# A two-layer attention trunk on one core: mask matmuls folded into the operands, scores in equal halves, and transposes and their evacuations moved ahead of the next tile's scores

## The reference

```python
# layer 0, group A (latent heads, width 64 + 32): query chunk must not be before key chunk
mask = key_chunk[None, :] <= q_chunk[:, None]            # chunks of 64
s = jnp.where(mask[None, None], s, NEG_INF)
# layer 0, group B (chunk heads, width 64): own chunk and the 8 before it
s = jnp.where(valid[None, None, :, None, :], s + bias[None, :, None], NEG_INF)
# layer 1 (fox heads, width 64): causal by token, with a decay
s = jnp.where(mask[None, None], s + cq[..., :, None] - cum[..., None, :], NEG_INF)
# all of them
pr = jax.nn.softmax(s, axis=-1)
o = pr @ v                                               # then a SiLU gate, one output projection
```

## Time and profile before

| | us |
|---|---|
| median of 3 runs | 1913.37 (1913.27 to 1915.61) |
| the profiled execution, its time | 1913.73 |
| its span, first to last instruction | 1911.9 |
| TensorE matmul busy | 1768.6 (93%) |
| VectorE busy | 952.7 (50%) |
| ScalarE busy | 835.6 (44%) |
| GpSimd busy | 105.6 (6%) |
| DMA, share of 16 engines | 39.6% in the main queue |

### The profile page before, as it was taken

How to read it: one execution, slowest core, us unless ns; L and a number is a source line. 1 busy time by engine, 2 the same in 40 slices (tenths; PEclk the granted TensorE clock), 3 DMA queues, 4 the chain that set the end, 5 groups by cost and what they waited for, 6 DMA issues and landing times. The chain is left out here.

```text
span 1911.9 us, 31893 instructions
## 1 busy us (share of the span) xinstructions
PE 1768.6 (93%) x12720; PEld 1628.7 (85%) x12720; DVE 952.7 (50%) x1812; ACT 835.6 (44%) x1708; POOL 105.6 (6%) x58
## 2 busy tenths in 40 slices
PE   5999788899999998999979999999989999889998
PEld 5999787787887777989979999998867777789898
DVE  5454465304777774253354444421067777832521
ACT  4433233315777773142252333312168888811410
POOL 0000000000121120000000000000002121100000
PEclk9999999999999999999989999999989999999999
DMA  6045457525445555101133344453265555251211
GB/s 187 23 161 162 121 153 211 156 73 168 133 122 148 142 131 177 51 28 56 45 111 110 122 133 123 122 148 99 83 161 137 140 134 144 79 181 35 70 64 39
DMA packets 178275, 223.94 MB, mean 117 GB/s; under 512 B 12760, under 2 KB 148200, under 8 KB 178128
## 3 DMA queue, kind: packets, MB, share of 16 engines
q1 hardware_dynamic: 177056, 218.43, 39.6%
q0 software_dynamic: 640, 2.62, 0.5%
q10 hardware_dynamic: 432, 0.85, 0.1%
HBM read 150.34 MB, written 77.29 MB: 119 GB/s over the span
## 5 line engine op out<-in xcount | busy, mean ns | idle before, releaser
L1617 PE MATMUL m_acc<-g_area,g_a_hi 128*128 128x256 f32 (+1 forms) x2560 | 479.8, 288 | 10.1 <-DVE g_area L202 5.6
L1617 PEld LDWEIGHTS m_acc<-g_area,g_a_hi 128*128 128x128 f32 x2560 | 404.6, 193 | 10.4 <-DVE g_area L202 5.7
L1617 PE MATMUL m_acc<-g_area,g_a_lo 128*128 128x256 f32 (+1 forms) x1280 | 366.4, 286 | 0.0
L1617 PEld LDWEIGHTS m_acc<-g_area,g_a_lo 128*128 128x128 f32 x1280 | 245.8, 192 | 0.0
L640 PE MATMUL pa_acc<-g_area,g_a_hi 128*128 128x256 f32 (+2 forms) x1024 | 208.2, 301 | 15.9 <-DVE g_area L202 15.9
L1617 PE MATMUL t_acc<-g_area,g_a_hi 128*128 128x256 f32 x1024 | 190.1, 286 | 5.1 <-DVE g_area L202 5.1
L640 PEld LDWEIGHTS pa_acc<-g_area,g_a_hi 128*128 128x128 f32 x1024 | 167.2, 195 | 16.4 <-issue 16.4
L202 DVE TENSOR_TENSOR g_area<-g_w_raw,g_area 128x2048 fp32r<-128x2048 f32 (+5 forms) x55 | 112.0, 2050 | 123.2 <-ACT g_area L196 123.2
L1617 PEld LDWEIGHTS t_acc<-g_area,g_a_hi 128*128 128x128 f32 x1024 | 160.7, 192 | 5.3 <-DVE g_area L202 5.3
L640 PE MATMUL pa_acc<-g_area,g_a_lo 128*128 128x256 f32 (+2 forms) x512 | 151.8, 297 | 0.0
L1042 PE MATMUL ab_scores<-g_area 96*128 96x512 f32 (+5 forms) x480 | 143.6, 380 | 3.8 <-PEq L102 3.8
(11 more groups left out here) (236 smaller groups left out, 3322.1 us busy)
## 6 DMA issues: line engine op xcount, KB each, us to landing
g_w_raw<-in_fox_w_in SPq DMA_DIRECT2D x16, 1024.0 KB, 6.0
g_area<-f_q SPq DMA_DIRECT2D x48, 256.0 KB
g_area<-f_k SPq DMA_DIRECT2D x48, 256.0 KB
g_w_raw<-in_ab_w_in SPq DMA_DIRECT2D x10, 1024.0 KB, 5.6
ab_v<-s_v SPq DMA_DIRECT2D x16, 512.0 KB, 3.5
g_w_raw<-in_pe_gate_w SPq DMA_DIRECT2D x8, 1024.0 KB, 5.3
f_v<-m_pr SPq DMA_DIRECT2D x32, 256.0 KB, 2.8
fox_v<-f_v SPq DMA_DIRECT2D x16, 512.0 KB, 3.5
```

Source lines behind the costliest of these rows:

```text
L1617: last = nc.tensor.matmul(dst, a[:, k, t * P:(t + 1) * P], w[:, k0 + k, 0:n], start=(k == 0 and a is m_hi and w is w_hi), stop=(k == kt - ...
```

## The change

Five things are changed.

1. *Latent masks.* Eight rows are added to the contraction (`MROWS` = 96 + 8): a row per block of 128 tokens, in q a 1 where the query is in the first half of its block, in k a -1e30 where the key is in the second half of the same block. They come from a DRAM tensor `m_chunk`, which `stage_ab` writes: VectorE makes the rows in the tile `y`, POOL stores them with four DMAs, and VectorE waits for those stores before its first evacuation overwrites `y`. `load_qk` issues 7 loads for a latent head instead of 4.
2. *Chunk masks.* They are written into the bias: two POOL DMAs put -1e30 from `far_off` over the corners of `s_bias`. The low part of q is loaded twice, so that the second matmul has 128 rows too (`load_qk` issues 6 loads instead of 5).
3. *Halves.* A tile of n columns is scored as one piece if n is at most 512, otherwise as two equal pieces of n / 2, one in each bank. The fox heads' `causal` matmul stays. Maxima, biases and exponentials read the two banks through a view with one more dimension.
4. *TensorE's order* in step s: `turn_p(s - 2)` before `score(s)`.
5. *VectorE's order* in step s: `evacuate(s - 2)` before `row_max(s)`. ScalarE's order stays.

The core of the diff:

```diff
-    QK_LOADS = {"mla": 4, "chk": 5, "fox": 7}
+    QK_LOADS = {"mla": 7, "chk": 6, "fox": 7}
...
             pairs = [(q[0:QK], qs[0]), (k[0:QK], ks[0]), (qx[0:QK], qs[1]), (kx[0:QK], ks[1])]
+            pairs += [(q[QK:MROWS], m_chunk[0]), (k[QK:MROWS], m_chunk[1]), (kx[QK:MROWS], m_chunk[1])]
...
+        if kind == "chk":
+            pairs += [(qx[64:P], qs[1])]
...
+                    pool.wait_ge(rows_made, 1)
+                    for m, (one_at, zero_at) in enumerate(((0, 1), (1, 0))):
+                        row = m_chunk[m].rearrange("r (t a n) -> r t a n", t=ST, a=2)
+                        pool.dma_start(row[:, :, one_at, :], rows_of[:, m, :].rearrange("r (t n) -> r t n", t=ST))\
+                            .then_inc(rows_stored, 16)
+                        pool.dma_start(row[:, :, zero_at, :], rows_of[:, 2, :].rearrange("r (t n) -> r t n", t=ST))\
+                            .then_inc(rows_stored, 16)
+                    pool.wait_ge(rows_stored, 64)
...
+                    for rows, cols in ((slice(0, CHUNK), slice(BAND - CHUNK, BAND)), (slice(CHUNK, P), slice(0, CHUNK))):
+                        pool.dma_start(s_bias[:, rows, cols].rearrange("h q n -> q h n"),
+                                       far_off[rows, :].unsqueeze(1).to_broadcast([CHUNK, HEADS, CHUNK])).then_inc(skewed, 16)
...
+                        if e == 0:
+                            dve.wait_ge(rows_stored, 64)
...
+        def in_banks(row, s):
+            n = (s % NT + 1 - lowest(s)) * P
+            many = 1 if n <= HALF else 2
+            return row.rearrange("q (c n) -> q c n", c=2)[:, 0:many, 0:n // many]
...
-                        for c in range(0, n, HALF):
-                            w = min(HALF, n - c)
-                            dst = scores[:, t % 2, c:c + w]
-                            keys = slice(lo * P + c, lo * P + c + w)
...
+                        if mla:
+                            terms = [(q, k, MROWS), (q, kx, MROWS), (qx, k, QK)]
+                        else:
+                            terms = [(q, k, P), (qx, kx if fox else k, 67 if fox else P)]
+                        dst = in_banks(scores[:, t % 2, :], s)
+                        w = dst.shape[2]
+                        for m, (a, kk, r) in enumerate(terms):
+                            for c in range(dst.shape[1]):
+                                keys = slice(lo * P + c * w, lo * P + (c + 1) * w)
+                                ins = nc.tensor.matmul(dst[:, c, :], a[0:r, b, rows], kk[0:r, b, keys], start=(m == 0),
                                                        stop=(m == len(terms) - 1))
-                                if m == 0:
-                                    for cols, mask in masks:
-                                        nc.tensor.matmul(dst[:, cols], ident_b[:], mask[:], start=False, stop=False)
+                            if fox and m == 0:
+                                nc.tensor.matmul(dst[:, dst.shape[1] - 1, w - P:w], ident_b[:], causal[:], start=False, stop=False)
...
                     for s in range(TILES + 5):
+                        if 0 <= s - 2 < TILES:
+                            turn_p(s - 2)
                         if s < TILES:
                             score(s)
-                        if 0 <= s - 2 < TILES:
-                            turn_p(s - 2)
...
                     for s in range(TILES + 6):
+                        if 0 <= s - 2 < TILES:
+                            evacuate(s - 2)
                         if s < TILES:
                             row_max(s)
                         if s >= 3 and s % 2 == 1 and s - 2 < TILES:
                             invert((s - 3) // 2)
-                        if 0 <= s - 2 < TILES:
-                            evacuate(s - 2)
```

More of the change, by code:

```diff
@@ L30 @@
 QK = NOPE + ROPE
+MROWS = QK + 8
 QLORA, KVLORA = 384, 256
@@ L875, in tables @@
                         link(nc.vector.tensor_tensor(kr[:].rearrange("q t n -> q (t n)"), t1[:, 0], t1[:, 1], ALU.add))
[L877 to L881, removed]
-                    nc.vector.memset(high_q[CHUNK:P, :], NEG)
-                    dve.wait_ge(made, 2)
+                    nc.vector.memset(far_off[:], NEG)
+                    dve.wait_ge(made, 2)
+                    nc.vector.tensor_copy(rows_of[:, 2, :].rearrange("r (t n) -> r t n", t=ST).bitcast(F32R),
+                                          ident[0:ST, CHUNK:P].unsqueeze(1).to_broadcast([ST, ST, CHUNK]))
+                    diagonal = ident[0:ST, 0:ST].unsqueeze(2).to_broadcast([ST, ST, CHUNK])
+                    nc.vector.tensor_copy(rows_of[:, 0, :].rearrange("r (t n) -> r t n", t=ST).bitcast(F32R), diagonal)
+                    nc.vector.tensor_scalar(rows_of[:, 1, :].rearrange("r (t n) -> r t n", t=ST).bitcast(F32R), diagonal, NEG,
+                                            None, ALU.mult).then_inc(rows_made, 1)
                     nc.vector.tensor_copy(ident_b[:], ident[:])
@@ L939, in stage_attention, with in_pieces @@
             qk_at[hd] = counts[hd % 2]
+        def in_banks(row, s):
+            n = (s % NT + 1 - lowest(s)) * P
+            many = 1 if n <= HALF else 2
+            return row.rearrange("q (c n) -> q c n", c=2)[:, 0:many, 0:n // many]
+        def in_pieces(row, s):
+            n = (s % NT + 1 - lowest(s)) * P
+            return row[:, 0:n].rearrange("q (c n) -> q c n", c=1 if n <= HALF else 2)
         def in_units(rows):
@@ L1011, in score @@
                         b, lo = hd % 2, lowest(s)
[L1012 to L1014 removed]
+                        mla = kinds[hd] == "mla"
                         if s == 0:
@@ L1022, in score @@
                             pe.wait_ge(maxed if is_chk[s - 2] else exped, s - 1)
-                        n = (t + 1 - lo) * P
                         rows = slice(t * P, (t + 1) * P)
-                        for c in range(0, n, HALF):
-                            w = min(HALF, n - c)
-                            dst = scores[:, t % 2, c:c + w]
-                            keys = slice(lo * P + c, lo * P + c + w)
-                            if mla:
-                                terms = [(q, k, KROWS), (qx, k, KROWS), (q, kx, KROWS)]
-                            else:
-                                terms = [(q, k, KROWS), (qx, kx if fox else k, XROWS)]
-                            masks = []
-                            if c + w == n:
-                                if chk:
-                                    masks.append((slice(w - CHUNK, w), low_q))
-                                else:
-                                    masks.append((slice(w - P, w), causal if fox else blockc))
-                            if chk and c == 0 and t >= BAND // P - 1:
-                                masks.append((slice(0, CHUNK), high_q))
-                            for m, (a, kk, r) in enumerate(terms):
-                                ins = nc.tensor.matmul(dst, a[0:r, b, rows], kk[0:r, b, keys], start=(m == 0),
@@ L1165, in row_max @@
                                 dve.wait_ge(in_x[b], 16 * ((hd - first_chk) // 2 + 1))
-                            nc.vector.tensor_tensor_reduce(out=prob[:, s % 3, 0:n], in0=scores[:, t % 2, 0:n],
-                                                           in1=extra[:, b, BAND - n:BAND], scale=-1.0, scalar=BIG,
+                            nc.vector.tensor_tensor_reduce(out=in_pieces(prob[:, s % 3, :], s),
+                                                           in0=in_banks(scores[:, t % 2, :], s),
+                                                           in1=in_pieces(extra[:, b, BAND - n:BAND], s), scale=-1.0, scalar=BIG,
                                                            op0=ALU.add, op1=ALU.min, accum_out=r).then_inc(maxed, 1)
```

20 lines of the change are left out of this document (10 added, 10 removed).

## The result

The changed kernel takes 2146.7 us (median of 4 runs, 2145.7 to 2147.6) where the kernel before takes 1913.3 on the same chip (4 runs, 1913.0 to 1915.6): a ratio of 1.122, 95% interval 1.120 to 1.124.

A forecast was written before the change was run, and what follows sets the result against it. TensorE was taken to set the attention stages' pace before, a VectorE-ScalarE round per tile after: 1913.7 + 247.5 (111.1 first stage, 136.4 fox) + 6 small waits = 2167 us, 13% slower; own range 2147 to 2201, to 2216 with the clock rival's lower part.

The forecast's parts named there:

- Every tile costs at least the sum: VectorE's new order makes a round through ScalarE span one tile instead of two: +247.5 us over the attention stages.
- M, X, Ea(s-1), Ed(s-1): Row maximum (VectorE), exponential (ScalarE), then the previous tile's evacuations: high part on ScalarE, remainder on VectorE.
- signs listed: Expected trace: VectorE and ScalarE waiting on each other, heads of 24 to 26 us, stages of 401 and 413, TensorE 60% busy.
- T: A tile's transposes on TensorE, which its evacuations wait for; ScalarE was to wait for them no longer.
- 0.12 more a tile: Gap on ScalarE behind the exponential, put down to the accumulator read: 0.96 us a head.
- The hand-over: Passing on a pair of heads on ScalarE (L1133): 1.07 us once in two heads, 0.54 a head.
- Small waits: Waits left out of the sum, such as the clock at stage starts or late transposes: 0 to 40 us, 6 taken.
- The range: The forecast's own range: 2147 us (steps 3% shorter, small waits of 10) to 2201.
- rival A: The round does not bind, so TensorE's savings count: 51 us faster, 1863 us; chance 0.05.
- T ahead of S: TensorE's new order, transposes before scores: worth nothing, the maximum and exponential covering the transposes' first piece.
- Rival B: TensorE's clock falls to 1.2 GHz and its work outlasts the round: at most 2311 us, 2215 for a third; chance 0.11.

The follow-up runs named there:

- dve_moved: The kernel before with only VectorE's order changed, evacuation of tile s-2 ahead of the maximum of tile s: 2149.8 us, ratio 1.125.
- dve_back: The changed kernel with only VectorE's order put back; masks, halves and TensorE's new order stay: 1996.1 us, ratio 1.042.
- far_behind: The changed kernel with ScalarE's copy to `far` moved behind the evacuation: 2055.7 us, ratio 1.074.
- best_far: The changed kernel with TensorE's and VectorE's orders put back and ScalarE's copy to `far` behind the evacuation: 1866.4 us, ratio 0.975.
- far_only: The kernel before with only ScalarE's copy to `far` moved behind the evacuation: 1898.7 us, ratio 0.992.
- pe_more: The changed kernel with each spread transpose on TensorE issued six times over, some 140 us more work: 2147.2 us, ratio 1.121.

## Why the prediction was right or wrong

**Right: the mechanism.** "Every tile costs at least the sum" of M, X, Ea(s-1), Ed(s-1) through VectorE's order: the order alone gives the loss (`dve_moved`), and putting it back takes 151 us away (`dve_back`). Of the signs listed most came: VectorE's wait for ScalarE (181.9 us in 129 waits, 1.4 each), ScalarE's for M, next to none for T, other stages unchanged within 2. The others were off: heads of 22.8 to 26.3 us after each stage's first where it said 24 to 26, stages of 393 and 405 where it said 401 and 413, and TensorE busy 73% and 75% of them, not 60%, in part because the clock fell and its matmuls took longer.

**Wrong: the size, by the term "0.12 more a tile".** It was read at 534.81 to 536.04, where the exponential is followed by the copy to `far`, and was charged to all tiles, "0.96 a head". Where the evacuation follows directly, nothing is lost: 0.57 from one start to the next for an exponential of 0.58 (601.54 to 602.11). The read of the accumulator, which the prediction gave as the reason, lies in both pairs. The steps of a latent head show it. Forecast by the terms, tiles 0 to 7: 2.63, 2.17, 2.01, 3.13, 3.00, 3.93, 3.69, 4.80. Measured, medians: 2.57, 2.17, 1.90, 3.13, 2.86, 3.94, 3.57, 4.79. The odd tiles, with the copy, are exact within 0.01; the even ones are 0.11 to 0.14 short, but for the first with 0.06 (in the fox heads it is 2.50, 0.13 short). 128 even tiles by 0.12 are 15.4 us of the 16.8 that the rounds came out short. `far_behind` shows it from the other side, by the 0.75 that the odd tiles lose. A gap behind an instruction belongs to the pair, and has to be read where the same pair stands; the earlier trace rows didn't hold that pair.

**The hand-over** was charged with its 1.07 and costs 0.95 (tile 1 takes 3.12 with it, 2.17 without, in the first stage), some 2 us in all. **Small waits:** 1.3 instead of 6. Rounds and waits together are 21.5 us, of which 20.5 show against 2167, since the profiled execution lies 1.0 below the median.

**The range.** Its low end took the steps 3% shorter but kept 10 us of small waits. The steps were 2.1% shorter (16.8 of 800) and the waits 1.3 us. Both bounds should have stood at their low ends together: 2137.

**Wrong: what is under the round.** "Were it gone they would be worth rival A", 1863, was tested by `dve_back` at 1996.1. The step that fails is the one on T ahead of S, "worth nothing here". In the changed kernel that holds; beneath it there is a round of TensorE with VectorE that costs 118.8 us by itself. The prediction followed VectorE's order through the other engines and didn't do the same for TensorE's. And with both orders back, masks and halves give 19.7 us and not the 51 summed for rival A: the matmuls did shrink as forecast (0.59 for the 640 columns, 0.6 estimated), but ScalarE's order took over as a bound. With the copy to `far` moved they give 32.2 (`best_far` against `far_only`), still not 51; that `best_far` as a whole gains 47.7 is no confirmation of rival A, which did not move the copy.

**Rival B** was partly right about its condition and wrong about its price. The granted clock did fall, to 0.88 and 0.86 on average, that is to its lower level for about a quarter of the time. By B's sum a third of the time was worth 48 us. The Trainium skill, TensorE: Matmul & The Clock Gate, section "A second HAM failure mode", has a kernel whose frequent small idles make the clock go to and fro, and the trace agrees that it does here. But TensorE's matmuls had slack in the round: against `pe_more` at 0.98 and 0.97 the spacing is 1.5 and 0.3 us longer. As the prediction said, the clock decides only from where TensorE's work passes the round. It did so at one step a head at most, from the first M to the second, where ScalarE then waits for the transposes:

```profile
571.66 0.60 ACT L1142 ACTIVATE g_area<-ab_turn 128x512 fp32r<-128x512 f32 x1 [0.26 <-PE ab_turn L1080]
```

Over that step the second to eighth latent head take 2.50 to 2.98 us in the changed kernel, at a granted clock between 0.50 and 0.75, and 2.50 each in `pe_more` at 1.00: 1.6 us in all, which is the difference in the first stage's spacing. It also makes the first tile of the latent heads the exception above.

## What to carry to other kernels

Before an instruction is moved on an in-order engine, follow the chain from each instruction that it is put in front of, through the other engines, back to it, and count the tiles that the chain spans: from two tiles to one meant 12% here, while no engine did more work. Do it for every engine whose order changes, since the longest round hides the others, and what is under it shows only when it is gone. Then look for what is in a round and needn't be: one copy moved behind the evacuation took 91 us off the slow kernel, 15.3 off the kernel before and 28.0 off the one with the masks folded.

## What was not expected of the hardware

- Going between matmuls of 128 and of 64 rows of contraction cost 0.13 to 0.14 us a change (1.35 to 0.83 us for four, 0.87 to 0.59 for two); at each the weight loads stopped for 0.2 us. Whether the 67-row and 104-row matmuls pay something like it was not measured.
- An evacuation behind an exponential with its accumulator read started at the recorded end of the exponential (1.10 of 1.11, 0.57 of 0.58), before the read was over; the copy to `far` in that place started 0.11 later (0.80 of 0.69), when it was (604.16 and 0.19, the copy at 604.37). Why these two differ stays open.
- A granted clock of 0.87 instead of 0.98 over 800 us of the two attention stages cost under 2 us, since the engine that it slows was off the round but for one step a head (up to 2.98 us instead of 2.50).
